# Decay exponents of an SSD mixer from running sums, with the step tables and the skip scaling moved between engines

## The chip, the cores and the metric

The kernel runs on one core of one Trainium2 chip. The metric is the device time of one execution in microseconds (us); lower is better. The core has TensorE (PE) for matrix products, VectorE (DVE), ScalarE (ACT) and GpSimd (POOL) for element-wise work, and SyncE (SP), which here issues the loads of weights. Each engine works through a queue of its own in program order; the queues are tied together by counting semaphores.

## The reference

Two transformer blocks run one after the other on 256 tokens of 1024 channels, all in float32. The first has a SwiGLU feed-forward, a mixer of pooling and windowed attention, and a second feed-forward. The second has a mixer of an SSD (state space) half and an MLA (latent attention) half that share one input product `u = h @ w_in`, then attention over 256 memory rows and a feed-forward with a convolution. The change touches the SSD half:

```
def ssd_mixer(u, ...):
    z, xbc, dt = jnp.split(u, ...)
    xbc = jax.nn.silu(causal_depthwise_conv(xbc, conv_w, conv_b))
    xs, bm, cm = jnp.split(xbc, ...)
    dt = jax.nn.softplus(dt + dt_bias)
    a_dt = dt * -exp(a_log)                     # per token and head, 16 heads
    a_cum = jnp.cumsum(a_dt, axis=-1)
    x_dt = xs * dt_c[..., None]
    cb = einsum("bclgn,bcsgn->bcgls", cm, bm)
    decay_in = exp(a_cum[l] - a_cum[s]) where s <= l, else 0
    y_diag = einsum("bcgls,bgecls,bcsgep->bclgep", cb, decay_in, x_dt)
    ...
    y = y_diag + y_off + xs * d_skip            # then * silu(z), then a norm per group
```

## The kernel before, in words

The kernel takes the 256 tokens as two tiles of 128 (`t` = 0, 1). Weights are read once, in units of 128 x 2048 (1536 for the unit `qup`). SP loads a unit into one of three `raw` buffers; ACT rounds it to `w_hi` (the helper `split` on ACT, L606), DVE stores the rest in `w_lo` (`split` on DVE, L1271), and TensorE forms each product of float32 accuracy from three single-pass products (L1963, L1964, L1965). The order of all work on each engine is written out by hand, with `wait_ge` and `then_inc` on named semaphores.

The region of the change is the end of the input product of the second block and the SSD work beside it. TensorE's order there is: 16 transposes of the convolved `xs` into `dn` (L2477); the second half of chunk 6 of the input product (`z_part(6, 1, t, ...)`, 24 products); the group products `C B^T` (L2489, 12 products of 128x128 in float32, in the order of `CB_ORDER`); chunk 7 of the input product cut in eight pieces (`z1_piece`, 6 products each) and laid between the decay work; two small products for the decay of a whole tile (`cum`, L2500 and L2501); and eight steps `i`, four head groups for each tile. A step is

- `step_rows(i)` on GpSimd (L1187): the lower triangle of ones times `a_dt` of four heads, 128x512, into `steps`;
- `decay_sums(i)` on TensorE (L2509): a float32 product `later` x `steps`, 128x512, which gives the exponents into PSUM bank `i % 2`;
- `decay_exp(i)` on ScalarE (L990): the exponential into `decay[i % 2]`;
- `decay_mask(i)` on VectorE (L1760): times the masked `C B^T` (`cbm`);
- `decay_out(i)` on TensorE (L2521): four float32 products with `xdt`.

`state_out` (L2530) follows step 3. VectorE gathers the results (L1774, L1778, L1783), which needs the skip term `xs * d_skip` that GpSimd makes in place in `xs_tok` (`skip(t)`, L1194), and GpSimd also makes `xd_end` (L1200). `xs_tok` itself is a copy by ScalarE (L972) from the transposes. `a_dt` comes out of a chain of small dependent operations on VectorE (`dt_and_x`, L1692 to L1703, 128x32 each; each of its links waits for the one before it). After the eight steps come the transposes of the MLA part (L1987, `norm("mla")`), their two halves `xT_hi` (ACT, L649) and `xT_lo` (DVE, L1312), and then the product with the units `qup` (`narrow`).

Of the kernel before, what the change touches and what calls it, by code (L numbers as in the profile page):

```python
# [23 lines left out]
F32 = mybir.dt.float32  # L24
# [115 lines left out]
NFREQ = ROT1 // 2 + ROT2 // 2  # L140
C_N = C_FREQ + NFREQ


def constants():
    c = np.zeros((P, C_N), np.float32)
    i = np.arange(P)
    c[:, C_ID:C_ID + P] = np.eye(P)
    c[:, C_TRI:C_TRI + P] = i[:, None] <= i[None, :]
    c[:, C_GT:C_GT + P] = i[:, None] > i[None, :]

    t = np.arange(S)
    for g, w in enumerate(POOL_WINDOWS):
        m = ((t[:, None] <= t[None, :]) & (t[:, None] > t[None, :] - w)) / np.minimum(t + 1, w)[None, :]
# [9 lines left out]
    c[:, C_FREQ:C_FREQ + NFREQ] = np.concatenate([f1, f2])[None, :]  # L163


    q = np.zeros((2, MH, S), np.float32)
    k = np.zeros((2, MH, S), np.float32)
    for t in range(TT):
        q[t, :, t * P:t * P + 64] = 1.0
        k[t, :, t * P + 64:(t + 1) * P] = NEG  # L170
    return c, np.stack([q, k]).reshape(2, 2, MH * S)


def two_blocks(nc, a, consts, mla_rows, out):
    with ExitStack() as ctx:
# [53 lines left out]
        with ExitStack() as under_arena:  # L229
# [92 lines left out]
        def bh(ap, n):  # L322
# [45 lines left out]
            "in2_act", "in2_dve", "xbT_ps", "conv_first", "conv_tap", "xbc_ready"))  # L368
        (dt_arg, dt_exp, adt_ready, dt_ready, cum_ps, cum_exp, cb_ps, cbm_ready) = map(sem, (
            "dt_arg", "dt_exp", "adt_ready", "dt_ready", "cum_ps", "cum_exp", "cb_ps", "cbm_ready"))  # L370
        (off_read, side_added, y0_read, zs_ready, skip_added) = map(sem, (
# [211 lines left out]
        def _(act):  # L583
# [400 lines left out]
            def decay_exp(i):  # L984

                act.wait_ge(dm_ps, i + 1)
                if i >= 2:
# [3 lines left out]
                               ACT.Exp).then_inc(dm_exp, 1)  # L991

            act.wait_ge(in2_dve, 6)
            squares("mla")
            z_out(6)
            split(U0["qup"])
            act.wait_ge(cum_ps, 1)
            act.activation(sm[:, 8, :], ps[:, 3, 384:416], ACT.Exp).then_inc(cum_exp, 1)
            decay_exp(0)
            decay_exp(1)  # L1000
            decay_exp(2)
            split(U0["qup"] + 1)
            for i in range(3, 6):
                decay_exp(i)
            z_out(7)
# [105 lines left out]
        def _(pool):  # L1111
# [67 lines left out]

            pool.wait_ge(adt_ready, 1)  # L1180
            adt = sm[:, 7, :].rearrange("p (t h) -> p t h", t=TT)

            def step_rows(i):
                if i >= 4:
                    pool.wait_ge(dm_ps, i - 3)
                t, g = i // SG, i % SG
                nc.gpsimd.tensor_tensor(steps[:, 4 * g:4 * g + 4, :], bh(tri, 4), bc(adt[:, t, 4 * g:4 * g + 4], P),  # L1187
                                        ALU.mult).then_inc(steps_ready, 1)
# [60 lines left out]
        def _(dve):  # L1249
# [429 lines left out]
            def dt_and_x():  # L1679
# [17 lines left out]
                for d in (15, 13, 11, 9, 7, 5, 3):  # L1697
# [65 lines left out]
            dve.wait_ge(cbm_ready, SG)  # L1763
            decay_mask(0)
            decay_mask(1)
            split(U0["qup"])
            decay_mask(2)
            decay_mask(3)
            split(U0["qup"] + 1)
            decay_mask(4)  # L1770
# [188 lines left out]
        def _(pe):  # L1959
# [518 lines left out]
            last.then_inc(xs_ps, 1)  # L2478
            for t in range(TT):
                z_part(6, 1, t, range(4))  # L2480

            pe.wait_ge(in2_act, 6)
            pe.wait_ge(in2_dve, 6)
            for g in CB_ORDER:
                if g == 0:

                    pe.wait_ge(in2_act, 7)
                for i, (s_, l_) in enumerate(((0, 0), (1, 1), (0, 1))):
# [271 lines left out]
```

## Time and profile before

| what | value |
|---|---|
| median of 3 runs | 1002.86 us (1002.82 to 1004.2) |
| the profiled execution | 1002.21 us, its span 1000.4 us |
| TensorE busy | 976.3 us, 98% of the span |
| VectorE busy | 617.5 us, 62% |
| ScalarE busy | 520.0 us, 52% |
| GpSimd busy | 67.9 us, 7% |
| granted TensorE clock | 0.999 of full speed |

The span is what the profiler sees from the first to the last instruction; 1.8 us lie around it. The busy time of TensorE is made of instructions that overlap: the duration of one runs from its issue to its modelled end, so the distance between two starts tells what one costs in a row of them. All times below that have the form 541.19 are microseconds from the start of the span.

### The profile page before, as it was taken

To read this page: it belongs to the slowest core of one execution; us is meant where nothing else is said; L and a number is where in the kernel's file an instruction comes from. 1 tells how busy PE (TensorE), PEld (TensorE's weight loads), DVE (VectorE), ACT (ScalarE), POOL (GpSimd) and SP (SyncE) were. 2 spreads that over 40 slices of the span, in tenths; PEclk is the share of its full clock that TensorE was granted. 3 is DMA by queue.
4 is the path that set the end of the run, shared out by engine and by line. 5 is a ranking of instruction groups with operands and counts; after the bars stand their busy time and mean duration, and the time that the engine had idled before them with its cause. 6 is when DMAs were issued, how large, how long until landed. Compare 5 with 4: busy or idle time off the path is not lost.

```text
span 1000.4 us, 13462 instructions
## 1 busy us (share of the span) xinstructions
PE 976.3 (98%) x5011; PEld 821.4 (82%) x5011; DVE 617.5 (62%) x769; ACT 520.0 (52%) x747; POOL 67.9 (7%) x100
## 2 busy tenths in 40 slices
PE   7999999999999999999999999999999999999996
PEld 5888888777878888887888788999999888888885
DVE  5545545665665545456678787675554666666766
ACT  7434343465564343444458286544453475555655
POOL 3300000000010000000001614000000000000000
PEclk9999999999999999999999999999999999999999
DMA  9956555623247565554544343224652526455541
GB/s 305 290 176 204 170 202 175 211 105 127 93 151 240 170 205 172 198 180 168 190 152 151 116 127 116 98 93 161 218 197 90 168 85 228 151 198 179 178 157 43
DMA packets 110169, 166.01 MB, mean 166 GB/s; under 512 B 5740, under 2 KB 83852, under 8 KB 109996
## 3 DMA queue, kind: packets, MB, share of 16 engines
q1 hardware_dynamic: 108032, 160.39, 47.1%
q0 software_dynamic: 1936, 5.00, 1.6%
q8 instruction: 27, 0.44, 0.2%
q10 hardware_dynamic: 160, 0.07, 0.0%
q14 instruction: 14, 0.11, 0.0%
HBM read 164.38 MB, written 1.05 MB: 165 GB/s over the span
## 4 chain that ended last, share of the span: by engine, by line
PE 86%; DVE 5%; ACT 4%; DMA 2%; POOL 1%; issue 1%; SPq 0%; POOLq 0%; ACTq 0%; DVEq 0%
PE ps L1963 25%; PE ps L1965 25%; PE ps L1964 25%; ACT w_hi L606 1%; DVE w_lo L1271 1%; PE ps L2271 1%; PE ps L2245 1%; PE ps L2177 1%; DVE arena L1730 1%; PE ps L2170 1%; DMA raw<-in_ffn_w_gu 1%; PE ps L1987 1%; PE ps L2509 1%; PE ps L2666 1%; POOL arena L1222 1%
## 5 line engine op out<-in xcount | busy, mean ns | idle before, releaser
L1271 DVE TENSOR_TENSOR w_lo<-raw,w_hi 128x2048 fp32r<-128x2048 f32 (+1 forms) x142 | 324.7, 2297 | 159.8 <-ACT w_hi L606 159.7
L1963 PE MATMUL ps<-w_hi,xT_hi 128*128 128x512 f32 (+2 forms) x898 | 349.3, 389 | 5.7 <-DVE xT_lo L1327 2.8
L1965 PE MATMUL ps<-w_hi,xT_lo 128*128 128x512 f32 (+2 forms) x898 | 340.2, 379 | 0.0
L1964 PE MATMUL ps<-w_lo,xT_hi 128*128 128x512 f32 (+2 forms) x898 | 339.8, 378 | 0.0
L606 ACT ACTIVATE w_hi<-raw 128x2048 fp32r<-128x2048 f32 (+1 forms) x142 | 267.7, 1898 | 67.4 <-PE ps L1965 58.3
L1963 PEld LDWEIGHTS ps<-w_hi,xT_hi 128*128 128x128 f32 x898 | 169.1, 188 | 39.1 <-issue 6.8
L1965 PEld LDWEIGHTS ps<-w_hi,xT_lo 128*128 128x128 f32 x898 | 169.0, 188 | 32.2
L1964 PEld LDWEIGHTS ps<-w_lo,xT_hi 128*128 128x128 f32 x898 | 169.3, 189 | 30.6 <-issue 1.4
L1963 PE MATMUL ps<-w_hi,hT_hi 128*128 128x512 f32 x224 | 87.8, 392 | 0.0
L1965 PE MATMUL ps<-w_hi,hT_lo 128*128 128x512 f32 x224 | 87.4, 390 | 0.0
L1964 PE MATMUL ps<-w_lo,hT_hi 128*128 128x512 f32 x224 | 87.4, 390 | 0.0
L719 ACT ACTIVATE arena<-ps,rstd 128x256 f32<-128x256 f32 x44 | 20.7, 474 | 60.7 <-PE ps L1965 60.7
L1963 PEld LDWEIGHTS ps<-w_hi,hT_hi 128*128 128x128 f32 x224 | 42.0, 188 | 10.3 <-DVE w_lo L1271 1.5
L1965 PEld LDWEIGHTS ps<-w_hi,hT_lo 128*128 128x128 f32 x224 | 42.1, 188 | 8.9
L1964 PEld LDWEIGHTS ps<-w_lo,hT_hi 128*128 128x128 f32 x224 | 42.1, 188 | 8.4
L1437 DVE SCALAR_TENSOR_TENSOR arena<-ps,conv_now,arena 128x255 f32<-128x255 f32 (+1 forms) x80 | 33.1, 476 | 24.5 <-ACT arena L745 24.1
L759 ACT ACTIVATE hT_hi<-ps 128x512 fp32r<-128x512 f32 x20 | 12.0, 598 | 68.6 <-PE ps L2177 68.6
L745 ACT ACTIVATE arena<-ps,conv_now 128x256 f32<-128x256 f32 x40 | 19.3, 564 | 35.9 <-PE ps L2170 35.9
L1963 PE MATMUL ps<-xT_hi,w_hi 128*128 128x256 f32 x128 | 36.8, 287 | 0.0
L1387 DVE SCALAR_TENSOR_TENSOR arena<-ps,rstd,arena 128x256 f32<-128x256 f32 x44 | 21.0, 481 | 25.4 <-ACT arena L719 25.4
L1965 PE MATMUL ps<-xT_hi,w_lo 128*128 128x256 f32 x128 | 36.3, 283 | 0.0
L1964 PE MATMUL ps<-xT_lo,w_hi 128*128 128x256 f32 x128 | 36.2, 283 | 0.0
(304 smaller groups left out, 1048.8 us busy)
## 6 DMA issues: line engine op xcount, KB each, us to landing
raw<-in_ffn_w_gu SPq DMA_DIRECT2D x86, 512.0 KB, 4.6
raw<-in_ffn_w_down SPq DMA_DIRECT2D x44, 512.0 KB, 3.9
raw<-in_w_ffn_up SPq DMA_DIRECT2D x44, 512.0 KB, 5.0
raw<-in_w_in SPq DMA_DIRECT2D x38, 512.0 KB, 4.6
raw<-in_w_out SPq DMA_DIRECT2D x24, 512.0 KB, 4.2
raw<-in_w_ffn_down SPq DMA_DIRECT2D x22, 512.0 KB, 4.2
raw<-in_w_mem_k SPq DMA_DIRECT2D x8, 512.0 KB, 3.9
raw<-in_w_mem_v SPq DMA_DIRECT2D x8, 512.0 KB, 4.8
```

Source lines behind the costliest of these rows:

```text
L606: act.activation(w_hi[HOME[k]][:, 0:n], raw[k % RING][:, 0:n], ACT.Copy).then_inc(rounded, 1)
L719: act.activation(silu_g[:, t, :], ps[:, t, 0:FC], ACT.Silu, scale=rstd[:, t, 0:1]).then_inc(silu_done, 1)
L745: act.activation(conv_y[:, q, :], ps[:, 2 + q // 2, q % 2 * S:q % 2 * S + S], ACT.Identity, bias=conv_now[:, 6 + q // 2, q % 2:q % 2 + 1], ...
L759: act.activation(hT_hi[:, :, :].rearrange("p a b -> p (a b)"), ps[:, 2, :], ACT.Copy).then_inc(hT_hi_done, 1)
L1222: last = TTp(v, x_, both(i), ALU.mult)
L1271: TTn(w_lo[HOME[k]][:, 0:n], raw[k % RING][:, 0:n], w_hi[HOME[k]][:, 0:n].bitcast(F32), ALU.subtract).then_inc(resid, 1)
L1387: STT(out=act_s[:, t, :], in0=ps[:, t, FC:2 * FC], scalar=rstd[:, t, 0:1], in1=silu_g[:, t, :], op0=ALU.mult, op1=ALU.mult).then_inc(s_rea ...
L1437: STT(out=conv_y[:, q, back:S], in0=src[:, 0:S - back], scalar=conv_now[:, 2 * tap + q // 2, q % 2:q % 2 + 1], in1=conv_y[:, q, back:S], o ...
L1730: STT(out=conv_x[:, q, back:S], in0=src[:, 0:S - back], scalar=cols[:, w:w + 1], in1=conv_x[:, q, back:S], op0=ALU.mult, op1=ALU.add).then ...
L1963: pe.matmul(out_, lh, rh, start=first, stop=False, **kw)
L1964: pe.matmul(out_, lh, rl, start=False, stop=False, **kw)
L1965: return pe.matmul(out_, ll, rh, start=False, stop=last, **kw)
```

## The change

The decay exponents of a step are no longer a float32 product with a table of `a_dt` under a triangle. Instead:

1. VectorE writes `a_dt` and `-a_dt` in four columns of blocks (`adt_cols`, four small operations more at the end of its chain), and TensorE multiplies them with the triangle once for each tile: the running sums `cumT` of all heads, transposed (two float32 products of 128x128, L2534 of the new kernel). They stand, with the two `cum` products, in the middle of the last part of chunk 6, ahead of its last six products.
2. ScalarE copies the sums rounded (`cumT_hi`) and from there into `cum_r` and `cum_l`; VectorE writes what the rounding left (`cumT_dve`, two operations of 32x256). The other rows of `cum_r` and `cum_l` are ones, set by GpSimd much earlier.
3. `step_rows(i)` now fills `cum_rhs` with the sums under a head's selector: GpSimd for tile 0 (four operations of 128x512), ScalarE for tile 1 (sixteen of 128x128, four behind each of the exponentials 0, 1, 2 and 3).
4. `decay_sums(i)` is now a bfloat16 product that sets the mask (-1e30 above the diagonal), and one single-pass product `cum_l` x `cum_rhs` added to it.
5. GpSimd scales both tiles of `xs_tok` (`skip`) ahead of its step tables, as soon as they are there.
6. ScalarE's squares for the MLA norm go behind the copies and `split(qup)`. VectorE's `split(qup)` goes from behind mask 1 to behind mask 3, and `split(qup + 1)` from behind mask 3 to ahead of mask 6.

```diff
+            act.wait_ge(cum_ps, 1)
+            act.activation(cumT_hi[:, :, :], ps[:, 3, 0:S].rearrange("p (a b) -> p a b", a=TT),
+                           ACT.Copy).then_inc(cumT_ready, 1)
+            act.activation(sm[:, 8, :], ps[:, 3, S:S + 2 * SH], ACT.Exp).then_inc(cum_exp, 1)
+            z_out(6)
+            act.wait_ge(cumT_ready, 1)
+            act.wait_ge(cum_ones, 3)
+            act.activation(cum_r[0:32, :, :], cumT_hi[0:32, :, :].bitcast(F32), ACT.Copy).then_inc(cumT_act, 1)
+            act.activation(cum_l[64:96, :, :], cumT_hi[64:96, :, :].bitcast(F32), ACT.Copy).then_inc(cumT_act, 1)
+            split(U0["qup"])
             act.wait_ge(in2_dve, 6)
             squares("mla")
-            z_out(6)
-            split(U0["qup"])
...
-            pool.wait_ge(adt_ready, 1)
...
+            for t in range(TT):
+                skip(t)
+            pool.wait_ge(cumT_act, 2)
+            pool.wait_ge(cumT_dve, 2)
+            def step_rows(i):
+                t, g = i // SG, i % SG
+                nc.gpsimd.tensor_tensor(cum_rhs[:, 4 * g:4 * g + 4, :], bh(cum_r[:, t, :].bitcast(F32), 4),
+                                        bc(heads[:, 4 * g:4 * g + 4], P), ALU.mult).then_inc(steps_ready, 1)
             for i in range(4):
                 step_rows(i)
...
-            skip(0)
-            for i in range(4, 8):
-                step_rows(i)
-            skip(1)
...
+                dve.wait_ge(adt_ready, 1)
+                dve.wait_ge(cum_ones, 1)
+                for b, sign in ((0, 1.0), (2, -1.0)):
+                    for i in range(2):
+                        nc.vector.tensor_scalar(adt_cols[:, :, b + i, 0:SH], rowt(7), sign, None,
+                                                ALU.mult).then_inc(adt_ready, 1)
...
+            split(U0["qup"] + 1)
             decay_mask(6)
             decay_mask(7)
...
-            for t in range(TT):
-                z_part(6, 1, t, range(4))
+            z_part(6, 1, 0, range(4))
+            z_part(6, 1, 1, range(2))
             pe.wait_ge(in2_act, 6)
             pe.wait_ge(in2_dve, 6)
+            pe.wait_ge(adt_ready, 5)
+            for t in range(TT):
+                pe.matmul(ps[:, 3, t * P:t * P + P], adt_cols[:, t, :, :].rearrange("p a b -> p (a b)"), tri,
+                          start=True, stop=True)
+            pe.matmul(ps[:, 3, S:S + SH], later, sm[:, 7, 0:SH], start=True, stop=True)
+            pe.matmul(ps[:, 3, S + SH:S + 2 * SH], tri, sm[:, 7, SH:2 * SH], start=True, stop=True).then_inc(cum_ps, 1)
+            z_part(6, 1, 1, range(2, 4))
...
-                pe.matmul(ps[:, i % 2, :], later, steps[:, 4 * g:4 * g + 4, :].rearrange("p a b -> p (a b)"),
-                          start=True, stop=True).then_inc(dm_ps, 1)
+                pe.matmul(ps[:, i % 2, :], mask_bf[:, P:2 * P], bh(ident_bf[:, :], 4), start=True, stop=False)
+                pe.matmul(ps[:, i % 2, :], cum_l[:, t, :], cum_rhs[:, 4 * g:4 * g + 4, :].rearrange("p a b -> p (a b)"),
+                          start=False, stop=True).then_inc(dm_ps, 1)
```

TensorE, from the last products of chunk 6 on. `arena` holds the activations and `sm` the small rows of dt; L2489 is `C B^T` before. Before:

```order
L1963 MATMUL ps<-w_hi,xT_hi 128x512
L1964 MATMUL ps<-w_lo,xT_hi 128x512
L1965 MATMUL ps<-w_hi,xT_lo 128x512
L2489 MATMUL ps<-arena 128x128 [waits in2_dve,in2_act]
L2489 MATMUL ps<-arena 128x128 x5
L2489 MATMUL ps<-arena 128x128 [waits in2_act]
L2489 MATMUL ps<-arena 128x128 x5
L1963 MATMUL ps<-w_hi,xT_hi 128x512 [waits resid,xdt_ready,xs_tok_ready]
```

The same place of the changed kernel, where L2012 to L2014 are the three products of a weight unit, L2534 the running sums and L2549 `C B^T`:

```order
L2014 MATMUL ps<-w_hi,xT_lo 128x512
L2534 MATMUL ps<-cst,arena 128x128 [waits adt_ready,in2_dve,in2_act]
L2534 MATMUL ps<-cst,arena 128x128
L2536 MATMUL ps<-sm,cst 128x16
L2537 MATMUL ps<-sm,cst 128x16
L2012 MATMUL ps<-w_hi,xT_hi 128x512 [waits resid]
L2013 MATMUL ps<-w_lo,xT_hi 128x512
L2014 MATMUL ps<-w_hi,xT_lo 128x512
L2012 MATMUL ps<-w_hi,xT_hi 128x512
L2013 MATMUL ps<-w_lo,xT_hi 128x512
L2014 MATMUL ps<-w_hi,xT_lo 128x512
L2549 MATMUL ps<-arena 128x128 x3
```

Four products and a wait for `adt_ready` now stand ahead of the last six products of chunk 6; the `cum` products stood behind chunk 7's second piece before.

GpSimd's queue before, from the norm of the input product to that of the MLA part (L1187 the step tables, L1200 `xd_end`, L1194 the skip scaling):

```order
L1187 TENSOR_TENSOR arena<-cst,sm 128x512 [waits adt_ready]
L1187 TENSOR_TENSOR arena<-cst,sm 128x512 x3
L1200 TENSOR_TENSOR xd_end<-arena,sm 128x1024 [waits cum_exp,xdt_ready]
L1194 TENSOR_TENSOR arena<-arena,head_rows 128x1024 [waits xs_tok_ready]
L1187 TENSOR_TENSOR arena<-cst,sm 128x512 [waits dm_ps] x4
L1194 TENSOR_TENSOR arena<-arena,head_rows 128x1024 [waits xs_tok_ready]
```

and in the changed kernel (L1226 the skip scaling, L1235 the step tables of tile 0):

```order
L1216 MEMSET arena 128x256
L1218 MEMSET cum_r 64x256 [waits cum_ones]
L1220 MEMSET cum_l 64x256 [waits cum_ones]
L1226 TENSOR_TENSOR arena<-arena,head_rows 128x1024 [waits xs_tok_ready] x2
L1235 TENSOR_TENSOR cum_rhs<-cum_r,cst 128x512 [waits cumT_dve,cumT_act]
L1235 TENSOR_TENSOR cum_rhs<-cum_r,cst 128x512 x3
L1242 TENSOR_TENSOR xd_end<-arena,sm 128x1024 [waits cum_exp,xdt_ready]
```

The two skip operations were behind the step tables and wait now for the copies of `xs_tok` alone.

VectorE's queue of the changed kernel around the last masks (L1811 a mask, L1822, L1826 and L1831 the gathering that was L1774, L1778 and L1783, L1309 `split`, L1350 `xT_lo`):

```order
L1811 TENSOR_TENSOR arena<-arena 128x512 [waits dm_exp]
L1822 TENSOR_TENSOR arena<-ps,arena 128x1024 [waits skip_ready,y_ps]
L1811 TENSOR_TENSOR arena<-arena 128x512 [waits dm_exp]
L1826 TENSOR_TENSOR arena<-ps,sm 128x1024 [waits cum_exp,off_ps]
L1831 TENSOR_TENSOR arena<-arena 128x1024 [waits skip_ready,off_read]
L1309 TENSOR_TENSOR w_lo<-raw,w_hi 128x1536 [waits rounded]
L1811 TENSOR_TENSOR arena<-arena 128x512 [waits dm_exp] x2
L1350 SCALAR_TENSOR_TENSOR xT_lo<-ps,cols,xT_hi 128x256 [waits xt_hi] x5
```

The same queue was, before, without the `w_lo` operation between the gathering and the last two masks.

## Rows read from the trace of the kernel before

**Rows 1.** The page: the span, and TensorE's busy time and instructions.
```profile
span 1000.4 us, 13462 instructions
PE 976.3 (98%) x5011; PEld 821.4 (82%) x5011; DVE 617.5 (62%) x769; ACT 520.0 (52%) x747; POOL 67.9 (7%) x100
```

**Rows 2.** Timeline of TensorE, 541 to 552: start, duration, line, idle before.
```profile
541.19 1.91 PE L2477 MATMUL ps<-cst,arena 128*128 128x128 f32 x16
542.85 0.48 PE L1963 MATMUL ps<-w_hi,xT_hi 128*128 128x512 f32 x1
...
548.39 3.12 PE L2489 MATMUL ps<-arena 128*128 128x128 f32 x24
551.26 0.47 PE L1963 MATMUL ps<-w_hi,xT_hi 128*128 128x512 f32 x1
```

**Rows 3.** Timeline of TensorE, 571 to 581.
```profile
571.06 1.02 PE L2509 MATMUL ps<-arena,cst 128*128 128x512 f32 x2
...
574.14 1.08 PE L2509 MATMUL ps<-arena,cst 128*128 128x512 f32 x2
575.05 1.00 PE L2521 MATMUL ps<-arena 128*128 128x64 f32 x8
575.89 1.08 PE L2509 MATMUL ps<-arena,cst 128*128 128x512 f32 x2
576.80 1.25 PE L1987 MATMUL ps<-cst,arena 128*128 128x128 f32 x10
577.90 1.90 PE L2521 MATMUL ps<-arena 128*128 128x64 f32 x16
580.79 0.47 PE L1963 MATMUL ps<-w_hi,xT_hi 128*128 128x512 f32 x1 [1.00 <-issue]
```

**Rows 4.** Timeline of ScalarE: the two copies of xs_tok.
```profile
543.13 1.94 ACT L972 ACTIVATE arena<-ps 128x1024 f32<-128x1024 f32 x2 [0.50 <-PE ps L2477]
```

**Rows 5.** Timeline of VectorE, 544 to 549: the end of the dt chain.
```profile
544.35 1.56 DVE L1698 SCALAR_TENSOR_TENSOR sm<-sm 128x32 f32<-128x32 f32 x7
...
546.39 0.19 DVE L1703 SCALAR_TENSOR_TENSOR sm<-sm 128x32 f32<-128x32 f32 x1
546.50 2.35 DVE L1708 TENSOR_TENSOR arena<-ps,sm 128x1024 f32<-128x1024 f32 x2
```

**Rows 6.** Timeline of GpSimd, 546 to 568.
```profile
546.66 4.03 POOL L1187 TENSOR_TENSOR arena<-cst,sm 128x512 f32<-128x512 f32 x4 [68.80 <-DVE sm L1703]
554.99 1.91 POOL L1200 TENSOR_TENSOR xd_end<-arena,sm 128x1024 f32<-128x1024 f32 x1 [4.29 <-ACT sm L998]
556.85 2.35 POOL L1194 TENSOR_TENSOR arena<-arena,head_rows 128x1024 f32<-128x1024 f32 x1
...
565.57 2.35 POOL L1194 TENSOR_TENSOR arena<-arena,head_rows 128x1024 f32<-128x1024 f32 x1
```

**Rows 7.** Timeline of VectorE, 556 to 582.
```profile
556.30 1.14 DVE L1760 TENSOR_TENSOR arena<-arena 128x512 f32<-128x512 f32 x1 [1.93 <-ACT arena L990]
...
566.08 3.45 DVE L1271 TENSOR_TENSOR w_lo<-raw,w_hi 128x1536 fp32r<-128x1536 f32 x1
569.46 0.68 DVE L1760 TENSOR_TENSOR arena<-arena 128x512 f32<-128x512 f32 x1
...
574.61 1.23 DVE L1783 TENSOR_TENSOR arena<-arena 128x1024 f32<-128x1024 f32 x1
...
578.64 2.05 DVE L1312 SCALAR_TENSOR_TENSOR xT_lo<-ps,cols,xT_hi 128x256 fp32r<-128x256 f32 x5 [0.31 <-ACT xT_hi L649]
581.10 1.76 DVE L1271 TENSOR_TENSOR w_lo<-raw,w_hi 128x1536 fp32r<-128x1536 f32 x1 [0.41 <-ACT w_hi L606]
```

**Rows 8.** Timeline of TensorE at 227: a bfloat16 mask product of the first block.
```profile
227.08 0.39 PE L2312 MATMUL ps<-mask_bf,ident_bf 128*128 128x512 bf16 x1
227.40 1.16 PE L2316 MATMUL ps<-arena 64*128 64x128 f32 x8
```

**Rows 9.** Timeline of TensorE at the start of the span.
```profile
5.39 1.97 PE L2010 MATMUL ps<-cst,X 128*128 128x128 f32 x8
```

More of the change, by code:

```diff
@@ L140 @@
 NFREQ = ROT1 // 2 + ROT2 // 2
-C_N = C_FREQ + NFREQ
+C_HEAD = C_FREQ + NFREQ
+C_N = C_HEAD + SH
 def constants():
@@ L236, in two_blocks @@
                 w_lo.append(under_arena.enter_context(nc.sbuf_tensor(f"spare_lo{i}", [P, UW], F32R)))
+        with ExitStack() as under_arena:
+            under_arena.enter_context(nc.sbuf_tensor("below_cum", [P, 11616], F32))
+            cum_rhs = under_arena.enter_context(nc.sbuf_tensor("cum_rhs", [P, SH, P], F32R))
+            under_arena.enter_context(nc.sbuf_tensor("below_cumT", [P, 2816], F32))
+            cumT_hi = under_arena.enter_context(nc.sbuf_tensor("cumT_hi", [P, TT, P], F32R))
+            under_arena.enter_context(nc.sbuf_tensor("below_cum_r", [P, 1536], F32))
+            cum_r = under_arena.enter_context(nc.sbuf_tensor("cum_r", [P, TT, P], F32R))
+            cum_l = under_arena.enter_context(nc.sbuf_tensor("cum_l", [P, TT, P], F32R))
         arena = sb("arena", [P, 18784])
@@ L277, in two_blocks @@
         y_ssd = view(16224, TT, D)
+        adt_cols = view(16224, TT, 4, 32)
         qT2 = view(0, MH, S)
@@ L368, in two_blocks @@
             "in2_act", "in2_dve", "xbT_ps", "conv_first", "conv_tap", "xbc_ready"))
-        (dt_arg, dt_exp, adt_ready, dt_ready, cum_ps, cum_exp, cb_ps, cbm_ready) = map(sem, (
-            "dt_arg", "dt_exp", "adt_ready", "dt_ready", "cum_ps", "cum_exp", "cb_ps", "cbm_ready"))
+        (cum_ones, cumT_ready, cumT_act, cumT_dve, steps_act) = map(sem, (
+            "cum_ones", "cumT_ready", "cumT_act", "cumT_dve", "steps_act"))
+        (dt_arg, dt_exp, adt_ready, cum_ps, cum_exp, cb_ps, cbm_ready) = map(sem, (
+            "dt_arg", "dt_exp", "adt_ready", "cum_ps", "cum_exp", "cb_ps", "cbm_ready"))
         (off_read, side_added, y0_read, zs_ready, skip_added) = map(sem, (
@@ L991, in decay_exp @@
                                ACT.Exp).then_inc(dm_exp, 1)
+            def step_rows(i):
+                g = i % SG
+                for h in range(4 * g, 4 * g + 4):
+                    last = act.activation(cum_rhs[:, h, :], cum_r[:, i // SG, :].bitcast(F32), ACT.Copy,
+                                          scale=heads[:, h:h + 1])
+                last.then_inc(steps_act, 1)
+            act.wait_ge(cum_ps, 1)
[8 more added lines that the diff above has]
+            split(U0["qup"])
             act.wait_ge(in2_dve, 6)
             squares("mla")
-            z_out(6)
-            split(U0["qup"])
-            act.wait_ge(cum_ps, 1)
-            act.activation(sm[:, 8, :], ps[:, 3, 384:416], ACT.Exp).then_inc(cum_exp, 1)
+            act.wait_ge(cumT_act, 2)
+            act.wait_ge(cumT_dve, 2)
             decay_exp(0)
+            step_rows(4)
             decay_exp(1)
+            step_rows(5)
             decay_exp(2)
+            step_rows(6)
             split(U0["qup"] + 1)
-            for i in range(3, 6):
-                decay_exp(i)
+            decay_exp(3)
+            step_rows(7)
+            decay_exp(4)
+            decay_exp(5)
             z_out(7)
@@ L1178, in _ @@
             norm("in2")
-            pool.wait_ge(adt_ready, 1)
[L1181 to L1188, printed above, removed]
+            nc.gpsimd.memset(adt_cols[:, :, :, :], 0.0).then_inc(cum_ones, 1)
+            pool.wait_ge(cum_ones, 1)
+            nc.gpsimd.memset(cum_r[64:128, :, :].bitcast(F32), 1.0).then_inc(cum_ones, 1)
+            pool.wait_ge(cum_ones, 2)
+            nc.gpsimd.memset(cum_l[0:64, :, :].bitcast(F32), 1.0).then_inc(cum_ones, 1)
             def skip(t):
@@ L1704, in dt_and_x @@
                     op1=ALU.mult).then_inc(adt_ready, 1)
-                for t in range(TT):
+                dve.wait_ge(adt_ready, 1)
[4 more added lines that the diff above has]
+                                                ALU.mult).then_inc(adt_ready, 1)
+                for t in range(TT):
+                    if t:
+                        dve.wait_ge(cumT_ready, 1)
+                        dve.wait_ge(cum_ones, 3)
+                        dve.wait_ge(cum_exp, 1)
+                        for at, to in ((32, cum_r), (96, cum_l)):
+                            TTn(to[at:at + 32, :, :], ps[at:at + 32, 3, 0:S].rearrange("p (a b) -> p a b", a=TT),
+                                cumT_hi[at:at + 32, :, :].bitcast(F32), ALU.subtract).then_inc(cumT_dve, 1)
                     dve.wait_ge(xs_tok_ready, t + 1)
@@ L1763, in _ @@
             dve.wait_ge(cbm_ready, SG)
-            decay_mask(0)
-            decay_mask(1)
+            for i in range(4):
+                decay_mask(i)
             split(U0["qup"])
-            decay_mask(2)
-            decay_mask(3)
-            split(U0["qup"] + 1)
             decay_mask(4)
@@ L2487, in _ @@
                     pe.wait_ge(in2_act, 7)
+                if g == 3:
+                    pe.wait_ge(cum_exp, 1)
+                    pe.wait_ge(cumT_dve, 2)
                 for i, (s_, l_) in enumerate(((0, 0), (1, 1), (0, 1))):
```

11 lines of the change are left out of this document (6 added, 5 removed).

## The prediction

> **What bounds the kernel now.** I read the page first. TensorE is busy 98% of the span [rows 1], so only what shortens TensorE's own list, or its waits, moves the end. I then read the timelines of the four engines side by side from 541 to 581, which is where every edit lies. The reader is to see three things in them.
>
> First, TensorE runs without a hole from the transposes at 541.19 to the last decay products at 577.90 [rows 2, 3]; the only wait is at the end. The last two sets of decay products (L2521) start at 577.90 and cost 0.84 us each (575.05 to 575.89), so they are through at 579.58, and the next product starts at 580.79 [rows 3]: 1.21 us, of which the profile shows 1.00 as idle. What comes last there is VectorE's `xT_lo`, 578.64 plus 2.05, thus 580.69 [rows 7].
>
> Second, dt's chain ends at 546.58 (546.39 plus 0.19) on VectorE [rows 5]. Nothing on TensorE waited for it before: its first reader there was `cum`, behind 551.26.
>
> Third, VectorE and GpSimd hinder each other. A mask takes 0.68 us alone (569.46); the one at 556.30 took 1.14, and ended at 557.44, 0.54 after GpSimd's `xd_end` had ended (554.99 plus 1.91 is 556.90) [rows 6, 7]. `w_lo` of 128x1536 takes 1.76 alone (581.10); the one at 566.08 took 3.45, until 569.53, which is 1.61 after the skip scaling at 565.57 had ended (567.92). So the VectorE operation stands still while GpSimd's runs, and then does its whole work. GpSimd yields likewise: the skip at 556.85 took 2.35 where `xd_end`, of the same size, took 1.91 with nobody beside it. They take turns, one whole instruction each. What is not hindered is an operation of VectorE with one operand in PSUM: `xdt` at 546.50, two in 2.35 us, ran beside four step tables of 1.0 us each (4.03 for four), and neither is stretched [rows 5, 6].
>
> **The change, part by part.** The sum is made against the profiled execution, 1002.21 us, of which the span is 1000.4.
>
> *The wait for dt.* TensorE comes to the running sums after 18 of the 24 products that begin at 542.85. The 24 take 5.54 us (to 548.39), 0.231 each [rows 2], so it arrives at 547.0. With the chain undisturbed `adt_ready` would reach 5 at about 547.1: 546.58, and four small operations at the chain's pace of about 0.1 when independent, the last one some 0.2 long. That is a stall of 0.1. But the two skip scalings now start as soon as ScalarE has copied `xs_tok`, and the first copy is there at about 544.15, the second at 545.07 (543.13 plus 1.94 for both) [rows 4]. The chain's seven operations L1698 start at 544.35 [rows 5], each reads two rows of `sm` in SBUF, as the hindered masks and `w_lo` read two operands in SBUF. A skip alone costs 1.8 us (565.57 to 567.92 is 2.35, of which it waited for the mask before it; the undisturbed `xd_end` took 1.91) [rows 6]. The first skip holds the chain from 544.35 to about 546.05, 1.7 us. The first L1698 then runs, the second skip takes its turn in the gap between two dependent operations, and holds the chain for another 1.75. So the chain ends 3.45 later, at 550.0, and the columns at 550.5: TensorE stands 3.5 us. The bounds are 0.1 (operations of 32 elements slip through) and 3.9 (two times 1.91 and the 0.1).
>
> The Trainium skill ("SBUF — State Buffer", section "SBUF: two separate sides") says the same as a rule without a size: GpSimd and a VectorE operation with two SBUF inputs exclude each other for a whole instruction, whoever is first. By it the chain waits for both skips and the stall is 3.5; [rows 6, 7] agree for operations of 512 and more elements, and no row shows the small ones. By the one reading the total below is +1.8, by the other -1.6.
>
> *The running sums.* Two float32 products of 128x128 are new. Twelve such products cost 2.87 us (548.39 to 551.26; the records count two for each) [rows 2], 0.24 each: +0.5. The `cum` products move and cost the same.
>
> *The steps.* A float32 `decay_sums` costs 0.91 us (574.14 to 575.05) [rows 3], eight cost 7.3. The new pair is a bfloat16 product, whose next neighbour starts 0.32 later (227.08 to 227.40) [rows 8], and a single-pass one at 0.23: 0.54 to 0.55. The other bound is two single-pass products in a train, 0.46. I take 0.54, since those rows show just this mask product ahead of one of another kind: -3.0 for eight, down to -3.6.
>
> *Behind the sums.* `C B^T` of group 3 now waits for `cum_exp` and VectorE's residuals. From the end of `cum` (0.84 after the wait ends) ScalarE needs about 0.9 and VectorE 0.8 more; TensorE has six products (1.4) and the first group (0.7) in between, 2.1 in all. It is hidden, by some 0.2 to 0.4. GpSimd's tables follow 4.3 us behind the sums, and the first step comes 7.4 us behind them. ScalarE's sixteen copies, at most 0.4 each, fall in the holes between exponentials; a step with a z piece lasts 2.7 us, and exponential, four copies and mask take less. Both cost nothing; without that cover each table would be 1.0.
>
> *The last masks.* Here the moved `split(qup + 1)` is exposed. From the start of sums 5 (571.06) to the end of the gathering on VectorE (574.61 plus 1.23) it is 4.8 us now [rows 3, 7], 4.4 with the shorter product. Then come 1.7 for the `w_lo` operation (1.76 alone) and 0.7 for mask 6: 6.8. TensorE has, from the same start, 0.54, a piece of 1.4, two sets of decay products of 0.84, two sums of 0.54, and 1.1 for the ten transposes (576.80 to 577.90): 5.7. So `decay_out(6)` waits for 1.1 us. In the kernel before mask 6 was done at 576.57, ahead of 577.90.
>
> *The last wait.* It stays. Behind mask 6 VectorE has mask 7 and 2.05 of `xT_lo`, 2.7; TensorE two sets, 1.7. 1.0 is open where 1.21 was: -0.2. A wait of 0.2 at group 0 of `C B^T` nearly goes: -0.1. The loads for `kvup` start later, behind the moved `w_lo` operations, but are wanted only behind three units of `qup`, 12 us of TensorE.
>
> *Sum.* 3.5 (new stall) + 0.5 - 3.0 + 1.1 - 0.3 = +1.8 us. The profiled execution becomes 1004.0. It is 0.65 under the median of the runs, so the median becomes 1002.86 + 1.8 = 1004.7. I go a little under it, 1004.4, since the term of the steps can only be larger on the gaining side. Everything later waits on TensorE's order and shifts with it.
>
> **The rivals.** *A: the small operations are not held.* For it: no row shows one of 32 elements beside GpSimd. Against it: the masks and `w_lo`, 0.7 and 1.8 long, were held by full GpSimd instructions. The sum is 0.1 + 0.5 - 3.0 + 1.1 - 0.3 = -1.6, and with the cheaper steps -2.2: 1000.7 to 1001.3. This is the case on the faster side; it decides if the first L1698 and its followers run through by 546.6.
>
> *B: only one skip holds the chain,* because the chain outruns the second, or holds its turn. Then the stall is 1.75 and the sum about 0: 1002.8.
>
> *C: the stall lets TensorE's clock fall.* After 5.2 us without work at the start, eight transposes took 1.97 [rows 9], where sixteen took 1.91 at 541.19 [rows 2]: half the pace. If a hole of 3.5 us did the same for as long as it lasted itself, it would add about 1.8: +3.6, thus 1006.5. Against it: the hole is shorter than that one. The Trainium skill ("TensorE: Matmul & The Clock Gate", section on the two states) has the clock fall to 1.2 GHz after idleness; by it this case is open.
>
> *D: a new wait behind the sums* (residuals or tables late, or ScalarE behind the exponentials), 0.5 to 2 us on top: 1005 to 1006.5.
>
> **How the numbers follow.** About 0.2% (2.0 us) is what a measurement of this kernel can tell from no change. My forecast (both skips hold, 3.5 us of stall) has 0.62, A 0.15, B 0.08, C 0.07, D 0.08. The forecast's own span is +1.2 (steps at 0.46) to +2.6 (0.4 more of stall, and 0.4 of stretched tables or masks), so about a third of it lies over +2.0. Slower: 0.2 + 0.07 + 0.05 = 0.32. Faster: A reaches -2.0 in less than half its cases, with a little for unseen gains: 0.09. The rest, 0.59, is within. The range from 1001.2 to 1006.2 leaves out about half of A and most of C.
>
> **What would show it.** In the changed kernel's trace: one L1736 of the dt chain that lasts over 1 us, twice, while L1226 runs; TensorE idle 3.5 us ahead of L2534, released by L1747; the pair L2568 and L2569 at 0.54 from start to start; a wait of about 1.1 ahead of the seventh set of L2581, with L1309 before its mask; 1.0 ahead of L2012 behind it. If TensorE's wait ahead of L2534 is under 0.5 the forecast is wrong by its largest term, and the kernel is faster by 1.6 or more.

## The result, and the profile after

The changed kernel takes 1006.67 us in the median of 11 runs (1004.4 to 1010.14); the kernel before, beside it, 1002.61 (1002.36 to 1004.2). The ratio is 1.0038, with a 95% interval of 1.0028 to 1.0047: slower by 4.1 us, where I had said 1.8, and the median is 0.5 above my range. The runs lie wide apart: 1004.4 at a granted clock of 0.999, 1005.8 at 0.997, 1008.2 at 0.994, 1010.14 at 0.991. The profiled run is one of 1005.75.

The page of the changed kernel:

```profile
span 1004.0 us, 13501 instructions
...
PE 975.6 (97%) x5015; PEld 821.9 (82%) x5015; DVE 619.2 (62%) x775; ACT 525.6 (52%) x766; POOL 62.6 (6%) x99
```

Against [rows 1] the span is 3.6 us longer (1000.4 before), with TensorE's busy time 0.7 lower (976.3 before). The time is in TensorE's waits and in the pace of its products.

GpSimd's timeline, then that of VectorE (start, duration, line), for the rows that answer to [rows 5, 6]:

```profile
544.19 3.77 POOL L1226 TENSOR_TENSOR arena<-arena,head_rows 128x1024 f32<-128x1024 f32 x2 [65.35 <-ACT arena L987]
```

```profile
544.33 4.81 DVE L1736 SCALAR_TENSOR_TENSOR sm<-sm 128x32 f32<-128x32 f32 x7
...
549.62 0.19 DVE L1741 SCALAR_TENSOR_TENSOR sm<-sm 128x32 f32<-128x32 f32 x1
549.85 0.44 DVE L1747 TENSOR_SCALAR arena<-sm 128x32 f32<-128x32 f32 x4
```

The chain of work that ended last takes two of the seven apart:

```profile
544.33 1.83 DVE sm L1736
546.18 1.84 DVE sm L1736
```

The seven operations took 1.56 us before and take 4.81 now, and 1.83 and 1.84 of it are two of them that stand still beside the two skip scalings: one turn each, as in the forecast. TensorE's timeline around the running sums:

```profile
546.75 0.39 PE L2014 MATMUL ps<-w_hi,xT_lo 128*128 128x512 f32 x1
550.43 0.73 PE L2534 MATMUL ps<-cst,arena 128*128 128x128 f32 x4 [3.29 <-DVE arena L1747]
550.95 0.45 PE L2536 MATMUL ps<-sm,cst 128*128 128x16 f32 x2
551.25 0.59 PE L2537 MATMUL ps<-sm,cst 128*128 128x16 f32 x2
551.67 0.77 PE L2012 MATMUL ps<-w_hi,xT_hi 128*128 128x512 f32 x1
552.25 0.63 PE L2013 MATMUL ps<-w_lo,xT_hi 128*128 128x512 f32 x1
...
553.95 0.58 PE L2014 MATMUL ps<-w_hi,xT_lo 128*128 128x512 f32 x1
554.37 3.12 PE L2549 MATMUL ps<-arena 128*128 128x128 f32 x24
```

The wait is there: 546.98 (546.75 and the 0.23 that a product costs) to 550.43, 3.45 us, of which the profile shows 3.29 as idle. And behind it the six products of chunk 6 take 2.70 us (551.67 to 554.37), 0.45 each, where they take 0.23 in [rows 2]. The windows say why (columns: stretch, its length, busy time of PE, PEld, DVE, ACT, POOL with counts, granted clock, DMA share, GB/s):

```profile
547.00:550.40 3.40, 0.14 (x1) 0.00 (x0) 3.09 (x14) 0.00 (x0) 0.96 (x1) 1.00 0.02 8
550.40:554.40 4.00, 3.97 (x15) 3.42 (x16) 2.88 (x4) 0.47 (x2) 0.00 (x0) 0.57 0.00 0
554.40:560.00 5.60, 5.58 (x37) 4.80 (x35) 4.54 (x10) 5.26 (x13) 3.36 (x3) 1.00 0.00 1
```

The granted clock is 0.57 over the four microseconds behind the hole, which is 1.2 GHz for most of them, and 1.00 again behind. The later places, for [rows 3]:

```profile
560.11 0.39 PE L2568 MATMUL ps<-ident_bf,mask_bf 128*128 128x512 bf16 x1
560.15 0.58 PE L2569 MATMUL ps<-cum_rhs,cum_l 128*128 128x512 f32 x1
560.57 0.39 PE L2012 MATMUL ps<-w_hi,xT_hi 128*128 128x512 f32 x1
...
578.85 1.25 PE L2036 MATMUL ps<-cst,arena 128*128 128x128 f32 x10
581.16 2.00 PE L2581 MATMUL ps<-arena 128*128 128x64 f32 x16 [1.05 <-DVE arena L1811]
583.77 0.47 PE L2012 MATMUL ps<-w_hi,xT_hi 128*128 128x512 f32 x1 [0.61 <-issue]
```

A pair of the new step costs 0.46 from start to start, and the wait for mask 6 is there: 1.2 us, of which the profile shows 1.05 as idle.

So every wait that I had forecast came, at its place and in its size, and the time is still wrong. What was open was the part above +1.8.

### The profile page after: what moved, and what is told of

It is laid out like the page before. It is cut to its first block, busy times and chain, and to the rows that moved or that the text cites. A ratio compares the mean times of both kernels' runs of the same rounds, so it can differ in the third digit from the quotient of the medians.

```text
span 1004.0 us, 13501 instructions
## 1 busy us (share of the span) xinstructions
PE 975.6 (97%) x5015; PEld 821.9 (82%) x5015; DVE 619.2 (62%) x775; ACT 525.6 (52%) x766; POOL 62.6 (6%) x99
## 3 DMA queue, kind: packets, MB, share of 16 engines
HBM read 164.39 MB, written 1.05 MB: 165 GB/s over the span
## 4 chain that ended last, share of the span: by engine, by line
PE 83%; DVE 8%; ACT 4%; DMA 2%; POOL 1%; issue 1%; SPq 0%; POOLq 0%; ACTq 0%; DVEq 0%
PE ps L2012 24%; PE ps L2014 24%; PE ps L2013 24%; DVE w_lo L1309 2%; DVE arena L1781 2%; ACT w_hi L621 1%; PE ps L2320 1%; PE ps L2294 1%; PE ps L2226 1%; PE ps L2219 1%; POOL arena L1260 1%; PE ps L2726 1%; DMA raw<-in_ffn_w_gu 1%; PE ps L2750 1%; DVE xT_lo L1365 1%
## 5 line engine op out<-in xcount | busy, mean ns | idle before, releaser
L1309 DVE TENSOR_TENSOR w_lo<-raw,w_hi 128x2048 fp32r<-128x2048 f32 (+1 forms) x142 | 322.7, 2282 | 160.0 <-ACT w_hi L621 159.9
L2012 PE MATMUL ps<-w_hi,xT_hi 128*128 128x512 f32 (+2 forms) x898 | 347.3, 387 | 5.4 <-DVE xT_lo L1365 2.9
L2014 PE MATMUL ps<-w_hi,xT_lo 128*128 128x512 f32 (+2 forms) x898 | 340.4, 379 | 0.0
L2012 PEld LDWEIGHTS ps<-w_hi,xT_hi 128*128 128x128 f32 x898 | 169.4, 189 | 37.7 <-issue 5.1
L2014 PEld LDWEIGHTS ps<-w_hi,xT_lo 128*128 128x128 f32 x898 | 169.2, 188 | 32.5
L2012 PE MATMUL ps<-w_hi,hT_hi 128*128 128x512 f32 x224 | 87.7, 392 | 0.0
L2014 PE MATMUL ps<-w_hi,hT_lo 128*128 128x512 f32 x224 | 87.3, 390 | 0.0
L2012 PEld LDWEIGHTS ps<-w_hi,hT_hi 128*128 128x128 f32 x224 | 42.0, 188 | 10.2 <-DVE w_lo L1309 1.5
L2014 PEld LDWEIGHTS ps<-w_hi,hT_lo 128*128 128x128 f32 x224 | 42.1, 188 | 8.9
L2012 PE MATMUL ps<-xT_hi,w_hi 128*128 128x256 f32 x128 | 36.7, 287 | 0.0
L2014 PE MATMUL ps<-xT_hi,w_lo 128*128 128x256 f32 x128 | 36.2, 283 | 0.0
```

The costliest lines, as they stand in the source:

```text
L1309: TTn(w_lo[HOME[k]][:, 0:n], raw[k % RING][:, 0:n], w_hi[HOME[k]][:, 0:n].bitcast(F32), ALU.subtract).then_inc(resid, 1)
L2012: pe.matmul(out_, lh, rh, start=first, stop=False, **kw)
L2014: return pe.matmul(out_, ll, rh, start=False, stop=last, **kw)
```

## The experiments

My theory after the result: a hole on TensorE (a stretch in which it waits) makes its clock fall for some microseconds behind it (the rival C of the prediction, which I had at 0.07). Its rivals: R1, the clock falls because the new steps are lighter work for TensorE; R2, dt's chain was late for another reason than GpSimd; R3, what is above +1.8 comes from other waits, loads for instance. The kernel before ran beside the experiments: 1002.5 in the median of 29 runs (1001.89 to 1004.21) beside the first four, 1002.29 of 27 beside the last four, with clocks of 0.998 and 0.999 in nearly all.

**The skips behind `xd_end`.**

```diff
-            for t in range(TT):
-                skip(t)
             pool.wait_ge(cumT_act, 2)
...
                                     bc(sm[:, 8, 0:SH], SP_), ALU.mult).then_inc(xd_end_ready, 1)
+            for t in range(TT):
+                skip(t)
```

> The changed kernel with both skip scalings back behind xd_end on GpSimd; nothing else moves. My theory (the skips hold the dt chain on VectorE, this makes a hole of 3.3 us on TensorE, and the hole makes TensorE's clock fall): the seven L1736 take 1.6 us in all again, the wait ahead of the running sums is under 0.3 us, the granted clock is back at 0.999 in every run, and the time is 1.3 to 2.2 us below the kernel before (about 1001.0), with a spread as small as that one's. Rival R1 (the clock falls because the new steps are lighter work for TensorE): the hole goes, but the clock stays at 0.991 to 0.997 and the times spread over some us. Rival R2 (small operations were late for a reason other than GpSimd): the chain stays at 4.8 us.

Measured: 1001.03 us (1000.43 to 1003.39, 11 runs), ratio 0.9988 (0.998 to 0.9997). The wait for dt is gone, and the seven L1736 take 1.55 us again, so R2 falls. Six runs lie at 1000.43 to 1001.03, where I had them; the other five at 1002.22 to 1003.39. Of these the profiled one, 1003.39, has a clock of 0.995; the four others have 0.997 to 0.999, so that a fall is not certain in them. This is neither mine as I put it nor R1, since the windows show where the clock fell:

```profile
571.00:574.00 3.00, 3.00 (x24) 2.73 (x23) 2.97 (x4) 1.86 (x3) 0.00 (x0) 1.00 0.15 63
574.00:577.00 3.00, 1.95 (x18) 1.72 (x16) 3.00 (x4) 2.69 (x7) 0.00 (x0) 1.00 0.08 19
577.00:580.00 3.00, 2.50 (x15) 2.15 (x14) 3.00 (x6) 2.97 (x3) 0.00 (x0) 0.67 0.90 326
580.00:583.00 3.00, 3.00 (x9) 2.33 (x8) 2.97 (x4) 1.53 (x2) 0.00 (x0) 0.50 0.46 141
583.00:586.00 3.00, 3.00 (x11) 2.40 (x10) 1.64 (x7) 0.00 (x0) 0.00 (x0) 0.70 0.62 213
```

There are no new steps behind 577, and none of the earlier ones ran at the low clock. In finer stretches it is 1.00 up to 577.9 and 0.50 from 578.1, and TensorE's timeline has the waits at either side of that:

```profile
576.24 2.11 PE L2581 MATMUL ps<-arena 128*128 128x64 f32 x16 [1.05 <-DVE arena L1811]
578.85 0.77 PE L2012 MATMUL ps<-w_hi,xT_hi 128*128 128x512 f32 x1 [0.50 <-issue]
579.41 0.63 PE L2013 MATMUL ps<-w_lo,xT_hi 128*128 128x512 f32 x1
579.84 0.63 PE L2014 MATMUL ps<-w_hi,xT_lo 128*128 128x512 f32 x1
```

The wait for mask 6 (1.05) is the second hole; the clock falls 1.8 us behind its end and ahead of the wait for `xT_lo` (0.50), so this one did not make it fall. In this one run the fall only follows the second hole; whether the hole makes it is tested below. It is the moved `split(qup + 1)` that makes the wait for mask 6: with it back, the wait is gone (fifth experiment).

**Fourteen products in the hole.** The skips stay at the front.

```diff
+            for r in range(14):
+                pe.matmul(ps[:, 3, :], w_hi[HOME[in2_unit0(6) + 1]][:, 0:P], xT_hi[:, 2 * (r % 4):2 * (r % 4) + 2, :].rearrange("p a b -> p (a b)"),
+                          start=True, stop=True)
             pe.wait_ge(adt_ready, 5)
```

> The changed kernel with 14 single-pass products of 128x512 into the PSUM bank of the running sums, directly ahead of the wait for dt (their result is overwritten); they fill about 3.2 us of the hole. My theory: dt comes no earlier, the step after it starts at the same time, but the clock stays at 0.999, so that the time is the unthrottled sum, 1.8 us above the kernel before (about 1004.4), spread under 1 us. Rival R1 (lighter steps): clock and times as in the changed kernel, about 1006.7 with a spread of 5 us. Rival R3 (what is above +1.8 comes from other waits, loads say): time about 1006.7 at a clock of 0.999.

Measured: 1005.96 us (1003.66 to 1007.47, 5 runs), ratio 1.0037 (1.0024 to 1.005). I missed the median, I think since the second hole is still in this kernel: clocks of 0.996, 0.995 and 0.995 in the three slowest runs. At the first hole the clock stayed; the profiled run:

```profile
547.00:550.00 3.00, 3.00 (x14) 2.28 (x13) 2.69 (x13) 0.00 (x0) 0.80 (x1) 1.00 0.00 0
550.00:553.00 3.00, 2.99 (x19) 2.56 (x19) 2.31 (x6) 0.70 (x3) 0.00 (x0) 1.00 0.00 0
```

By itself this experiment leaves open which hole costs how much. The profiled run (1003.66) also tells how a mean clock is to be read. Its mean is 0.998, and it is at the low clock only from 997.4 on, where TensorE has no more work; such a stretch stands at the end of every kernel here. So 0.998 by itself shows no fall that cost time, and does not exclude one: the next profiled run has 0.998 with one.

**One skip at the front.**

```diff
-            for t in range(TT):
-                skip(t)
+            skip(0)
...
                                     bc(sm[:, 8, 0:SH], SP_), ALU.mult).then_inc(xd_end_ready, 1)
+            skip(1)
```

> The changed kernel with the scaling of tile 0 at the front and that of tile 1 behind xd_end. My theory: one turn instead of two, so the seven L1736 take 3.2 us, the wait ahead of the running sums is 1.5 to 1.8 us, and without a fall of the clock the time is the kernel before's within 0.5 us (about 1002.7). If a hole of half the length makes the clock fall too, 1 to 3 us more. Rival (the chain would slip through after the first hold anyway): same time as with both at the front.

Measured: 1004.24 us (1002.1 to 1006.91, 12 runs), ratio 1.0013 (1.0003 to 1.0024). One turn, as expected:

```profile
545.26 3.18 DVE L1736 SCALAR_TENSOR_TENSOR sm<-sm 128x32 f32<-128x32 f32 x7
```

```profile
549.73 0.68 PE L2534 MATMUL ps<-cst,arena 128*128 128x128 f32 x4 [1.63 <-DVE arena L1747]
...
550.62 0.55 PE L2012 MATMUL ps<-w_hi,xT_hi 128*128 128x512 f32 x1
550.96 0.63 PE L2013 MATMUL ps<-w_lo,xT_hi 128*128 128x512 f32 x1
551.39 0.63 PE L2014 MATMUL ps<-w_hi,xT_lo 128*128 128x512 f32 x1
```

Five runs at a clock of 0.999 lie at 1002.1 to 1002.72, within 0.5 us of the kernel before; the other seven at 1004.1 to 1006.9 and 0.998 to 0.993. In the profiled one the products behind a hole of 1.6 us are 0.43 apart, and nothing is low behind its second hole. A hole half as long can be enough. That it does so less often is less sure, since this kernel has the second hole as well.

**The skips at the front of the kernel before**, nothing else (the definition of `skip` moves along with them).

```diff
+            for t in range(TT):
+                skip(t)
             pool.wait_ge(adt_ready, 1)
...
-            skip(0)
             for i in range(4, 8):
                 step_rows(i)
-            skip(1)
```

> The kernel before with one part of the change alone: both skip scalings at the front of GpSimd's region, ahead of the step tables. My theory: dt's chain is held for 3.3 us here too, but TensorE first wants something of it only at the eighth... at its first piece of chunk 7 (xdt, at 551.3 before, ready at about 552.4 now), so it costs about 1.2 us (1003.8) with no fall of the clock. If the early skips hurt by themselves whatever waits: +3.3. If they are harmless alone: 0.

Measured: 1003.47 us (1002.85 to 1005.52, 11 runs), ratio 1.0012 (1.0004 to 1.0021). The chain is held as in the changed kernel (its seven operations take 4.83 us), but TensorE waits only 0.7 for what hangs on it, at the first piece of chunk 7:

```profile
552.06 0.47 PE L1963 MATMUL ps<-w_hi,xT_hi 128*128 128x512 f32 x1 [0.72 <-issue]
```

Two of the eleven runs, 1004.8 and 1005.52, lie apart from the rest. The early skips alone cost 1 us; it takes TensorE's early need for dt to make 3.3 of it.

**Both undone: the skips late, and `split(qup + 1)` back ahead of mask 4.** To the diff of the first experiment comes

```diff
             split(U0["qup"])
+            split(U0["qup"] + 1)
             decay_mask(4)
...
-            split(U0["qup"] + 1)
             decay_mask(6)
```

> The changed kernel with both skips behind xd_end, and VectorE's split(qup + 1) back ahead of mask 4. My theory (there are two holes in which the clock can fall: the wait for dt, and the wait for mask 6 together with the one for xT_lo behind it): both holes but the last wait are gone, 1.0 to 1.3 us less than with the late skips alone, 999.6 to 1000.0, at a clock of 0.998 to 0.999 in nearly every run. Rival R1 (the clock falls because the new steps are lighter work): clocks of 0.995 and less in some runs as before, and a spread of 3 us.

Measured: 1000.31 us (999.59 to 1002.43, 12 runs), ratio 0.9976 (0.9966 to 0.9985): faster than both kernels. Ten of twelve runs lie at 999.59 to 1000.8, with clocks of 0.998 and 0.999; the two others are 1001.31 (0.996) and 1002.43 (0.998). The new steps run in it as they do in the changed kernel, and the low clocks are gone in ten of twelve runs, which R1 does not explain. TensorE's timeline: 0.2 us at most ahead of the sums (547.73 to 547.90), no wait for mask 6, and the last wait is what it was in [rows 3].

```profile
547.90 0.68 PE L2534 MATMUL ps<-cst,arena 128*128 128x128 f32 x4
...
574.72 1.25 PE L2036 MATMUL ps<-cst,arena 128*128 128x128 f32 x10
575.81 1.90 PE L2581 MATMUL ps<-arena 128*128 128x64 f32 x16
578.71 0.47 PE L2012 MATMUL ps<-w_hi,xT_hi 128*128 128x512 f32 x1 [1.00 <-issue]
```

**`split(qup + 1)` alone back**, the skips at the front (the last diff alone).

> The changed kernel with split(qup + 1) alone back ahead of mask 4; the skips stay at the front. My theory: no wait for mask 6, so 1.0 to 1.3 us off the unthrottled time (1003.2 to 1003.5 as the lowest), and the falls of the clock that the first hole causes stay: median 1004.5 to 1006, granted clock 0.995 to 0.999. If the second hole were the cause of most falls: median under 1004.

Measured: 1004.84 us (1003.22 to 1007.76, 9 runs), ratio 1.0024 (1.0014 to 1.0034). The one run at 0.999 has 1003.22, 1.2 under that of the changed kernel (1004.4); the eight others have 0.998 to 0.994, seven of them 0.997 or less. The first hole alone is enough for a fall in most runs.

**The same with the fourteen products** of the second experiment.

> The same with the 14 products ahead of the wait for dt. My theory: the hole is filled and the other one gone, so the clock stays, the times lie close together at 1003.3 to 1003.8, the unthrottled sum of +1.8 less the 1.1 for mask 6. If the products do not keep the clock up: as the one without them.

Measured: 1003.32 us (1002.54 to 1004.59, 11 runs), ratio 1.0007 (0.9998 to 1.0016), all at 0.998 or 0.999. dt is as late as in the kernel above, and TensorE does 14 products more, which nothing uses; it is 1.5 us faster in the median, and the spread is 2.0 where it was 4.5. The running sums start at nearly the same time, 550.58 (550.79 in the profiled run without the products, where dt's chain starts 0.14 later):

```profile
547.21 3.33 PE L2533 MATMUL ps<-xT_hi,w_hi 128*128 128x512 f32 x14
550.58 0.71 PE L2537 MATMUL ps<-cst,arena 128*128 128x128 f32 x4
...
551.50 0.48 PE L2012 MATMUL ps<-w_hi,xT_hi 128*128 128x512 f32 x1
551.81 0.39 PE L2013 MATMUL ps<-w_lo,xT_hi 128*128 128x512 f32 x1
```

Nothing in it shortens another wait, and its median lies where I had put the sum without the clock: R3 falls. The two kernels with the fourteen products also bear out that the second hole lowers the clock. They differ by the place of `split(qup + 1)` alone: with it moved three of five runs have 0.996 or 0.995, with it back none of eleven is under 0.998. (No trace of the three slow ones is kept, so where the clock fell in them is not shown.)

**The old steps with the hole.** The kernel before with the skips at the front (as in the fourth diff), its two `cum` products moved, and ScalarE's exponential of them ahead of `z_out(6)`.

```diff
             squares("mla")
+            act.wait_ge(cum_ps, 1)
+            act.activation(sm[:, 8, :], ps[:, 3, 384:416], ACT.Exp).then_inc(cum_exp, 1)
             z_out(6)
             split(U0["qup"])
-            act.wait_ge(cum_ps, 1)
-            act.activation(sm[:, 8, :], ps[:, 3, 384:416], ACT.Exp).then_inc(cum_exp, 1)
...
-            for t in range(TT):
-                z_part(6, 1, t, range(4))
+            z_part(6, 1, 0, range(4))
+            z_part(6, 1, 1, range(2))
             pe.wait_ge(in2_act, 6)
             pe.wait_ge(in2_dve, 6)
+            pe.wait_ge(adt_ready, 1)
+            pe.matmul(ps[:, 3, 384:400], later, sm[:, 7, 0:SH], start=True, stop=True)
+            pe.matmul(ps[:, 3, 400:416], tri, sm[:, 7, SH:2 * SH], start=True, stop=True).then_inc(cum_ps, 1)
+            z_part(6, 1, 1, range(2, 4))
             for g in CB_ORDER:
+                if g == 3:
+                    pe.wait_ge(cum_exp, 1)
...
-            pe.wait_ge(adt_ready, 1)
             pe.wait_ge(cbm_ready, 4)
-            pe.matmul(ps[:, 3, 384:400], later, sm[:, 7, 0:SH], start=True, stop=True)
-            pe.matmul(ps[:, 3, 400:416], tri, sm[:, 7, SH:2 * SH], start=True, stop=True).then_inc(cum_ps, 1)
```

> The kernel before, with its old float32 steps, with the skips at the front and its two cum products where the changed kernel has them, six products ahead of the end of chunk 6 (and the exponential of the sums ahead of z_out(6) on ScalarE). Nothing of the new arithmetic. My theory: the hole of about 3.1 us comes from the turns of GpSimd and the early wait alone: lowest time about 3.1 us above the kernel before (1005.6), and falls of the clock in most runs, median 1006.5 to 1008. Rival R1: a hole but no falls, all runs near 1005.6.

Measured: 1008.65 us (1005.7 to 1010.03, 6 runs), ratio 1.0051 (1.0036 to 1.0066). The lowest run, at 0.998, is 3.4 above the kernel before; five of six have clocks of 0.997 to 0.993. The median is 0.65 above my 1006.5 to 1008. No new step is in this kernel, so lighter steps are not what lowers the clock: R1 falls. The clock is low from the end of the hole on (it goes just ahead of 550, 0.3 us before the first product), until 556.7; in the changed kernel it was low until 554.3:

```profile
547.00:550.00 3.00, 0.38 (x2) 0.00 (x0) 2.73 (x10) 1.82 (x9) 1.17 (x1) 0.97 0.05 18
550.00:553.00 3.00, 2.83 (x9) 2.48 (x10) 2.29 (x3) 0.20 (x1) 2.90 (x3) 0.50 0.01 3
553.00:556.00 3.00, 3.00 (x14) 2.81 (x13) 0.62 (x2) 2.04 (x3) 2.99 (x3) 0.50 0.00 0
```

The same profiled run, 1010.03, has a second fall, behind the last wait, the one of [rows 3] that the kernel before has too:

```profile
586.80 0.47 PE L1963 MATMUL ps<-w_hi,xT_hi 128*128 128x512 f32 x1 [1.00 <-issue]
...
587.71 0.63 PE L1963 MATMUL ps<-w_hi,xT_hi 128*128 128x512 f32 x1
588.14 0.63 PE L1964 MATMUL ps<-w_lo,xT_hi 128*128 128x512 f32 x1
```

The products are 0.43 apart from 587.71 to 590.70, and the twelve from 586.80 on take 4.4 us instead of 2.8. So the last wait, 1.0 idle, can be followed by a fall as well; it was not in the other profiled runs that have it.

## Why the prediction was wrong, point by point

**The stall for dt** was forecast at 3.5 us and is 3.45, by the mechanism named: two small operations of the chain last 1.83 and 1.84 us, one beside each skip. The late skips take it away, one skip makes 1.6 of it, and the same skips do the same to the chain of the old kernel. That operations of 32 elements are held like long ones is shown; rival A falls, and rival B too. The section "SBUF: two separate sides" of the Trainium skill's page "SBUF — State Buffer" gives the port that GpSimd shares with a VectorE operation with two SBUF inputs to whoever starts first, for the whole instruction, and makes no exception for short ones. The trace agrees: an operation of about 0.2 us became one of 1.83.

**The running sums** cost 0.5 as forecast: 0.52 for the pair at full clock (547.90 to the next start at 548.42 in the fast kernel).

**The steps** gained more than I took: a pair costs 0.46, not 0.54, so -3.6 instead of -3.0. The 0.32 of [rows 8], where a float32 product stands behind the mask, is thus not what the mask costs ahead of a single-pass one.

**The last masks** were forecast at 1.1 and cost 1.2 (and the terms that I gave for TensorE there add up to 5.8, not 5.7, so that my own sum was 1.0). The kernel without the skips' hole and the one with neither differ by 0.7 in the median, and their fastest runs by 0.8; the pair with the skips at the front differs by 1.8 in the median and 1.2 at full clock.

**What failed** is the term for the clock behind the stall. The forecast had it at zero, and rival C, which had it, got 0.07 of the chances on the argument "the hole is shorter than that one". The experiment with one skip shows a fall behind a hole of half the length. [rows 9] was weak ground for either side: the profile has the granted clock at 1.00 from 5 to 10 us, so no row shows that those slow transposes were the clock. Rival C's own figure, 1006.5, is 0.2 from the median, and its mechanism is the one that the runs show, though the size was a guess from the length of the hole. The measured terms without it give 3.45 + 0.5 - 3.6 + 1.2 - 0.3 = +1.3; the one run of the changed kernel at 0.999 stands at +1.8 (0.3 of the rest may be a wait further on for a transfer of mask rows, 0.88 in the profiled run instead of 0.55; I did not test it), the median at +4.1. I put the difference of 2.3 down to the clock, and the experiments show it: filling the hole with useless products takes most of it away (1004.84 to 1003.32, and 0.994 to 0.998 as the lowest clock), taking the hole away does, and making the hole in the kernel before brings it. In the profiled run of the changed kernel the clock costs 1.6: from the running sums to `C B^T` it takes 3.94 us (550.43 to 554.37), and the kernel with both undone takes 2.36 (547.90 to 550.26). That the forecast of +1.8 equals the one run at 0.999 is in part luck: the measured terms give 0.5 less, and what makes up the difference is not shown.

**And there were two holes**, of which I had looked at the clock behind the first alone. In the profiled run without the first hole the clock fell behind the wait of 1.05 for mask 6 and was low from 578.0 to 584.8, which costs 2.6 us (13 products from 578.85 on, 0.43 apart instead of 0.23). How often it does so is not shown as well as behind the first. Without the first hole 5 of 11 runs lie 1.2 us or more above the cluster of the rest, and 2 of 12 lie 0.5 or more above it where the wait for mask 6 is gone too; with the first hole filled it is three low clocks in five runs against none in eleven. Nor is a kernel without it free of falls: of the 56 runs of the kernel before, whose last wait is 1.0, nine lie above 1003.4, five of them with a clock of 0.996 (one has 0.948; I did not look into it), and the last experiment's second fall stands behind just this wait.

**The range** reached to 1006.2 and the median is 0.5 over it; its upper end left out most of C on purpose. I had given 0.59 to a change too small to tell and 0.32 to slower; it is slower.

Left open: the best kernel gains 2.0 us in the median, while its region on TensorE, 543.55 to 578.71, is 2.8 shorter than [rows 2, 3] have it. Its region starts 0.7 later in the profiled run, and in the other kernels 0.2 earlier to 0.9 later, so the start moves from run to run; whether the rest is this I did not test.

## What to carry to other kernels

When a change makes TensorE wait, price the wait and then the clock behind it: here a hole of 3.3 us cost another 1.5 in the median by itself and 2.3 together with a second one of 1.05, and a kernel with holes of 1.6 and 1.05 kept its clock in 5 of 12 runs and lay 1.6 to 4.4 above the kernel before in the rest. A wide spread of times with a granted clock that goes down as they go up is the sign, and products that nothing uses, laid into the hole, are the test. And an element-wise GpSimd operation that is moved ahead "since its input is there" stops each small VectorE operation with two operands in SBUF that falls beside it: look at what chain runs there before moving it.

## What the runs showed of the hardware that I had not expected

Behind a wait of 1.6 us the clock fell to 1.2 GHz (products 0.43 apart) in some executions of a program and not in others. Waits of 1.0 to 1.05 us were followed by a fall in two profiled runs (that with the late skips, and the second fall of the last experiment) and by none in the eight others. The low clock lasted 3.3 us in the profiled run of the changed kernel (551.0 to 554.3), 6.8 in that with the late skips and in the last experiment, and 3.3 in the latter's second fall. The pair of a bfloat16 and a single-pass product, both of 512 columns, costs 0.46 us, no more than two single-pass products, which are 0.23 apart.
